# A hybrid attention and SwiGLU layer on one core: the input projection with tokens on the output partitions instead of head dimensions

## What is computed

```
h = rms_norm(x, attn_norm[l])
proj = jnp.einsum('bsd,de->bse', h, w_in[l])
mq, mk, mv, dq, dk, dv = jnp.split(proj, splits, axis=-1)
mq = rms_norm(mq.reshape(B, S, MOBA_HEADS, HEAD_DIM), moba_q_norm[l])
mk = rms_norm(mk.reshape(B, S, MOBA_HEADS, HEAD_DIM), moba_k_norm[l])
mq, mk = apply_rope(mq, cos, sin), apply_rope(mk, cos, sin)
...
x = x + jnp.einsum('bse,ed->bsd', mixed, w_out[l])
h = rms_norm(x, ffn_norm[l])
x = x + jnp.einsum('bsf,fd->bsd', jax.nn.silu(g) * u, w_down[l])
```

## Time and profile before

| what | value |
|---|---|
| three runs | 625.57 us median (624.17 to 625.68) |
| profiled execution | 624.43 us, of it 622.6 us from first to last instruction |
| granted TensorE clock, mean | 0.999, the upper of its levels |
| TensorE busy | 604.8 us (97%) |
| VectorE, ScalarE busy | 484.1 us, 311.5 us |
| attention and projection of the 8 pairs | to about 255 us of the span |

### The profile page before, as it was taken

The page is one execution under the profiler, slowest core; times in us unless marked ns, Lnnn a source line. Parts: engine busy times, 40 slices in busy tenths (PEclk is TensorE's granted clock), DMA queues, the critical chain, the costliest instruction groups (busy, mean ns, idle before and its releaser), DMA issues.

```text
span 622.6 us, 10404 instructions
## 1 busy us (share of the span) xinstructions
PE 604.8 (97%) x3774; PEld 516.1 (83%) x3774; DVE 484.1 (78%) x821; ACT 311.5 (50%) x533; POOL 28.1 (5%) x28
## 2 busy tenths in 40 slices
PE   6999999999999899999999999999999999999997
PEld 5867677776768576879999999999999998888886
DVE  4867777787687878688877887787877876999774
ACT  5354546363555454444644554536454465555551
POOL 0000000000000000000000000000000022154200
PEclk9999999999999999999999999999999999999999
DMA  8313041321404041503303432133222369699901
GB/s 318 87 65 124 1 135 24 111 67 69 124 12 136 4 164 67 177 29 138 145 26 134 137 113 91 69 136 136 80 94 99 136 158 257 189 189 207 168 35 67
DMA packets 32953, 70.31 MB, mean 113 GB/s; under 512 B 3344, under 2 KB 3728, under 8 KB 32912
## 3 DMA queue, kind: packets, MB, share of 16 engines
q1 hardware_dynamic: 26896, 58.22, 27.5%
q0 software_dynamic: 6016, 11.54, 10.5%
HBM read 63.45 MB, written 2.10 MB: 105 GB/s over the span
## 4 chain that ended last, share of the span: by engine, by line
PE 88%; DVE 7%; ACT 2%; issue 2%; DMA 1%; DVEq 0%; SPq 0%; ACTq 0%
PE ps L1472 26%; PE ps L1473 25%; PE ps L1474 25%; PE ps L1536 3%; PE ps L1549 2%; PE ps L1504 2%; PE ps L1566 1%; PE ps L1613 1%; DVE w_lo L953 1%; ACT probs L621 1%; PE ps L1574 1%; DVE w_lo L935 1%; PE ps L1795 1%; DMA ident<-ident 1%; DVE residual L1204 0%
## 5 line engine op out<-in xcount | busy, mean ns | idle before, releaser
L1472 PE MATMUL ps<-h_sum_parts,w_hi 128*128 128x256 f32 x432 | 120.6, 279 | 0.7 <-ACT q_kept L805 0.7
L1473 PE MATMUL ps<-h_sum_parts,w_hi 128*128 128x256 f32 x432 | 120.9, 280 | 0.0
L1474 PE MATMUL ps<-h_sum_parts,w_lo 128*128 128x256 f32 x432 | 120.5, 279 | 0.0
L1472 PE MATMUL ps<-h_parts,w_hi 128*128 128x512 f32 x192 | 81.5, 424 | 2.1 <-DVE h_parts L1070 1.8
L1472 PEld LDWEIGHTS ps<-h_sum_parts,w_hi 128*128 128x128 f32 x432 | 81.2, 188 | 0.9 <-ACT q_kept L805 0.9
L1473 PEld LDWEIGHTS ps<-h_sum_parts,w_hi 128*128 128x128 f32 x432 | 81.1, 188 | 0.0
L1474 PEld LDWEIGHTS ps<-h_sum_parts,w_lo 128*128 128x128 f32 x432 | 80.8, 187 | 0.0
L1474 PE MATMUL ps<-h_parts,w_lo 128*128 128x512 f32 x192 | 75.5, 393 | 0.0
L1473 PE MATMUL ps<-h_parts,w_hi 128*128 128x512 f32 x192 | 75.3, 392 | 0.0
L621 ACT ACTIVATE probs<-ps,small 128x128 f32<-128x128 f32 (+3 forms) x64 | 39.0, 614 | 51.8 <-DVE small L1016 51.8
L1472 PE MATMUL ps<-w_hi,hidden_parts 128*128 128x512 f32 x154 | 60.9, 396 | 0.0
(11 more groups left out here) (175 smaller groups left out, 1250.6 us busy)
## 6 DMA issues: line engine op xcount, KB each, us to landing
w_raw<-wt SPq DMA_DIRECT2D x61, 512.0 KB, 4.2
w_raw_odd<-wt SPq DMA_DIRECT2D x24, 512.0 KB, 4.2
w_raw_odd<-wt POOLq DMA_DIRECT2D x12, 512.0 KB, 8.5
down_raw<-wt SPq DMA_DIRECT2D x6, 512.0 KB, 11.2
w_raw<-wt POOLq DMA_DIRECT2D x5, 512.0 KB, 9.6
residual<-x SPq DMA_DIRECT2D x4, 512.0 KB, 5.0
q_rotated<-q_gained SPq DMA_DIRECT2D x32, 64.0 KB, 2.0
k_rotated<-k_gained SPq DMA_DIRECT2D x32, 64.0 KB, 2.0
```

The lines of the kernel that those rows point to most:

```text
L1472: nc.tensor.matmul(dst, lh, rh, start=start, stop=False, skip_group_check=True)
L1473: nc.tensor.matmul(dst, lh, rl, start=False, stop=False, skip_group_check=True)
L1474: return nc.tensor.matmul(dst, ll, rh, start=False, stop=stop, skip_group_check=True)
```

## The change

The projection is turned round. `project(p, tt, k)` now keeps a 128x128 piece of h (a block of 128 tokens) stationary and streams 384 weight columns, the q, k and v columns of a pair together. A pair takes 32 steps of 3 matmuls: four row blocks (`tt`) of 8 steps. Weights come in chunks of 768 numbers per partition, four to a pair, in a ring of five. The result has tokens on the partitions, so the sums of squares are a free-axis reduce on VectorE, v needs no transpose, and rotary is made with tables by token that hold the gains too. q and k are then transposed (`turn_q`, `turn_k`) and copied (`q_out`, `k_out`). The eight rotate DMAs, `mean_squares`, `spread_k`, `turn_v`, `v_scale` and the per-pair gains are gone. The filler runs about two row blocks further ahead: 18 steps of pair 1 stand before the first scores. The loops are written out. At the start x is transposed tile by tile between row blocks. Cut to its core:

```diff
+CH = KT // 2
+IN_CHUNKS = PAIRS * CH
+RING = 5
...
+def in_bank(p, tt):
+    return ((0, 1, 7, 6) if p == 0 else (0, 1, 7, 1))[tt]
...
+def chunk_load(g):
+    p, c = divmod(g, CH)
+    if g >= RING:
+        sp.wait_ge(w_lo, g - RING + 1)
+    sp.dma_start(RAWC[:, ring(g)], wt[3 * p:3 * p + 3, :, 2 * P * c:2 * P * (c + 1)].rearrange(
+        "j p n -> p j n")).then_inc(raw_c[ring(g)], 16)
...
+sp.dma_start(X[:, 0], x[0]).then_inc(x_in[0], 16)
+for g in range(CH):
+    chunk_load(g)
+for t in range(1, TT):
     sp.dma_start(X[:, t], x[t]).then_inc(x_in[t], 16)
...
+chunk_load(CH)
...
+def x_hi(tt, k):
+    act.wait_ge(x_turned, KT // 2 * tt + k // 2 + 1)
+    ins = nc.scalar.activation(H1[:, k, 0, tt * P:(tt + 1) * P], ps[:, 2 + k // 2, k % 2 * P:(k % 2 + 1) * P],
+                               ACT.Copy, scale=VEC[:, k:k + 1])
...
+def chunk_hi(g):
...
+        if c < CH - 1:
+            act.wait_ge(w_used, (CH - 1) * p + c + 1)
+        else:
+            act.wait_ge(pj_s, TT * (p + 1))
+    nc.scalar.activation(WHC[:, ring(g)].rearrange("p k (j n) -> p k j n", j=3),
+                         RAWC[:, ring(g)].rearrange("p j (k n) -> p k j n", k=2), ACT.Copy).then_inc(w_hi, 1)
...
+def qk_out(p, tt):
+    act.wait_ge(pj_s, TT * p + tt + 1)
+    if p >= 1:
+        act.wait_ge(red_s, p)
+    nc.scalar.activation(SQ[:, tt], ps[:, in_bank(p, tt), 0:2 * P].rearrange("p (j n) -> p j n", j=2),
+                         ACT.Square).then_inc(sq_s, 1)
+    if p >= 1:
+        act.wait_ge(rn_s, p)
+    nc.scalar.activation(QK[:, tt], ps[:, in_bank(p, tt), 0:2 * P].rearrange("p (j n) -> p j n", j=2),
+                         ACT.Copy).then_inc(qk_s, 1)
...
+def v_out(p, tt):
...
+    if p >= 2:
+        act.wait_ge(pv_s, p - 1)
+    nc.scalar.activation(VF[p % 2][:, tt], ps[:, in_bank(p, tt), 2 * P:3 * P], ACT.Copy,
+                         scale=XR[:, tt:tt + 1]).then_inc(v_s, 1)
...
+def q_out(t):
+    act.wait_ge(q_turn, t + 1)
+    if t >= 1:
+        act.wait_ge(sc_s, TT * t)
+    nc.scalar.activation(QF[:], ps[:, 2], ACT.Copy).then_inc(qf_s, 1)
...
+for k in range(KT):
...
+tables_out()
...
+for t in range(PAIRS - 1):
+    moba = t < MOBA_PAIRS
+    exps(t, 0, moba)
+    qk_out(t + 1, 1)
...
+    if t > MOBA_PAIRS:
+        o_squares(t - 1)
+    next_hi(t, 0)
+    exps(t, 1, moba)
...
+    exps(t, 2, moba)
+    if t + 2 < PAIRS:
+        next_hi(t, 1)
...
+        exps(t, 3, moba)
...
+    next_hi(t, 2)
+    next_hi(t, 3)
+    if t > MOBA_PAIRS:
+        mix_hi(t - 1, False)
+    qk_out(t + 1, 3)
+    v_out(t + 1, 3)
...
+    if t + 2 < PAIRS:
+        qk_out(t + 2, 0)
+    if moba:
+        mix_hi(t, True)
+    q_out(t + 1)
+    k_out(t + 1)
...
+def chunk_lo(g):
...
+    nc.vector.tensor_tensor(WLC[:, ring(g)].rearrange(view, j=3),
+                            RAWC[:, ring(g)].rearrange("p j (k n) -> p k j n", k=2),
+                            WHC[:, ring(g)].bitcast(F32).rearrange(view, j=3), ALU.subtract).then_inc(w_lo, 1)
...
+def rope(p):
+    dve.wait_ge(sq_s, TT * (p + 1))
+    nc.vector.tensor_reduce(SQS, SQ[:].rearrange("p t j (a e) -> p (t j a) e", a=2), AX.X,
+                            ALU.add).then_inc(red_s, 1)
+    dve.wait_ge(qk_s, TT * (p + 1))
...
+    nc.vector.tensor_tensor(RC[:].rearrange(heads, a=2), raw, TC[:].rearrange("p t j e -> p (t j) e").unsqueeze(
+        2).broadcast_to([P, 2 * TT, 2, HEAD]), ALU.mult).then_inc(rc_s, 1)
+    nc.vector.tensor_tensor(RN[:].rearrange(heads, a=2), raw, TS[:].rearrange("p t j e -> p (t j) e").unsqueeze(
+        2).broadcast_to([P, 2 * TT, 2, HEAD]), ALU.mult).then_inc(rn_s, 1)
+    if p >= 1:
+        dve.wait_ge(k_turn, p)
+    dve.wait_ge(rc_s, p + 1)
+    dve.wait_ge(rn_s, p + 1)
+    halves = "p t j (a h e) -> p (t j a) h e"
+    to, cos, sin = (v[:].rearrange(halves, a=2, h=2) for v in (QKR, RC, RN))
+    for h in range(2):
+        nc.vector.tensor_tensor(to[:, :, h], cos[:, :, h], sin[:, :, 1 - h], ALU.add).then_inc(rope_s, 1)
...
+def scales(p):
...
+    y = rsqrt(SQS, 16, 1.0 / HEAD, qk_newton, p, EX).rearrange("p (t j a) -> p t j a", t=TT, j=2)
+    dve.wait_ge(rope_s, 2 * (p + 1))
+    k_rows = QKR[:, :, 1].rearrange("p t (a e) -> p t a e", a=2)
+    nc.vector.tensor_tensor(k_rows, k_rows, y[:, :, 1].unsqueeze(3).broadcast_to([P, TT, 2, HEAD]),
+                            ALU.mult).then_inc(kn_s, 1)
+    if p >= 1:
+        dve.wait_ge(ex_s, p * 8)
+    nc.vector.tensor_scalar(RQ.rearrange("p (t a) -> p t a", a=2), y[:, :, 0], HEAD ** -0.5, None,
+                            ALU.mult).then_inc(rq_s, 1)
...
+tables(0)
+chunk_lo(5)
+chunk_lo(6)
+rope(0)
+chunk_lo(7)
 scales(0)
...
+for t in range(PAIRS - 1):
...
-    norm(t, 1, True)
+    next_lo(t, 0)
+    norm(t, 1, moba)
     maxima(t, 2)
...
+    if t > MOBA_PAIRS:
+        o_norm(t - 1)
+    if t + 2 < PAIRS:
+        next_lo(t, 1)
+        maxima(t, 3)
...
+    norm(t, 2, moba)
+    next_lo(t, 2)
...
+    norm(t, 3, moba)
+    next_lo(t, 3)
+    rope(t + 1)
     scales(t + 1)
...
+def project(p, tt, k):
+    g = CH * p + k // 2
+    pe.wait_ge(w_lo, g + 1)
+    if k == 0 and in_tenant(p, tt):
+        pe.wait_ge(qk_s, in_tenant(p, tt))
+        pe.wait_ge(v_s, in_tenant(p, tt))
+    if p == 0:
+        pe.wait_ge(hl, KT * tt + k + 1)
...
+        if (tt, k) == (3, 0):
+            pe.wait_ge(tab_ev, 3)
+    qs, w = slice(tt * P, (tt + 1) * P), (slice(None), ring(g), k % 2)
+    ins = product(ps[:, in_bank(p, tt), 0:3 * P], H1[:, k, 0, qs], H1[:, k, 1, qs], WHC[w], WLC[w],
+                  k == 0, k == KT - 1)
     if k == KT - 1:
+        ins.then_inc(pj_s, 1)
+    elif tt == TT - 1 and k % 2 == 1:
         ins.then_inc(w_used, 1)
...
+def turn_q(t):
+    pe.wait_ge(rope_s, 2 * (t + 1))
+    if t >= 1:
+        pe.wait_ge(ex_s, 8 * t)
...
+        ins = nc.tensor.transpose(ps[:, 2, tt * P:(tt + 1) * P], QKR[:, tt, 0], ident[:])
+    ins.then_inc(q_turn, 1)
...
+turn_gains()
+turn_x(0)
+first_rows(0, 0, 6)
+turn_x(1)
+first_rows(0, 6, KT)
+first_rows(1, 0, 6)
+turn_x(2)
+first_rows(1, 6, KT)
+turn_tables()
+first_rows(2, 0, 6)
+turn_x(3)
+first_rows(2, 6, KT)
+first_rows(3, 0, KT)
...
+fill(11)
+turn_q(0)
 fill(4)
...
+turn_k(0)
 fill(3)
...
     scores(t, 0)
-    fill(2)
-    turn_v(t)
-    fill(1)
+    fill(3 if t else 1)
     scores(t, 1)
-    turn_p(t, 0, True)
-    fill(4)
+    fill(3)
+    turn_p(t, 0, moba)
     scores(t, 2)
     fill(4)
-    turn_p(t, 1, True)
+    turn_p(t, 1, moba)
     scores(t, 3)
...
     fill(6)
-    turn_p(t, 2, True)
-    mean_squares(t + 1)
...
+    fill(3 if t < PAIRS - 2 else 2)
+    turn_p(t, 2, moba)
+    fill(4 if t < PAIRS - 2 else 2)
+    turn_p(t, 3, moba)
+    fill(3 if t < PAIRS - 2 else 2)
+    heads_out(t, 0, moba)
+    heads_out(t, 1, moba)
+    fill(2)
+    turn_q(t + 1)
+    fill(2)
+    turn_k(t + 1)
+    fill(2)
```

836 lines of the change are left out of this document (311 added, 525 removed).

## The result

The changed kernel takes **653.61 us** (median of 4 runs, 651.09 to 655.21); the kernel before, beside it on the same chip, 624.87 us (4 runs, 623.88 to 625.68). The ratio is 1.046, 95% interval 1.042 to 1.050: 28.7 us slower. The forecast was 644.0 us with a range of 630 to 652, so the direction was right and the time lies above the range. The four runs of the changed kernel spread along with their mean granted clock: 651.09 us at 0.995, 652.58 at 0.990, 654.64 at 0.986 and 655.21 at 0.984.

The account below looks back on a forecast made before the run. TensorE was taken to bind, the score-to-exponential chain right behind. Added to 624.43 us: start +9.8, pair 0 +0.7, pair 1 +0.5, pairs 2 to 4 +2.5, pair 5 +2.0, pair 6 +2.2, pair 7 +1.7: 644 us, range 630 to 652.

Parts of the forecast that it names:

- The rival in which TensorE goes on binding: Whole kernel: no waits at the scores, four pairs of 26.1 us and three of 25.3, 615 us; chance 0.10.
- The projection itself: In-projection: no change; 384 columns take 0.173 us, a pair's steps 16.6 us against 16.5.
- The rival of dearer columns: In-projection: 384 columns take 0.187 us, a step costs 0.042 us more, 652 us in all; chance 0.11.
- The removed sums: Sums of squares taken off TensorE: 1.70 us a pair, 13.6 us in eight pairs.
- A moba pair: First scores to the next pair's first scores: 28.4 us against 27.9, the saved 1.7 eaten by 2.2 of waits.
- From the fourth scores to the next pair's first ... 18.0: End of a moba pair on TensorE: 22 steps (11.4 us), 6.1 and one more transpose group (0.45), against 16.77 before.
- The start: Up to pair 0's first scores: they come at 46.1 us, 9.8 later than before.
- The wait for chunk 7: Start: VectorE runs pair 0's rotary before chunk 7's split, done at 38.7; TensorE needs it at 36.1, waits 2.6 us.
- 18 steps of lead return nothing: Pair 1 steps (9.3 us) done before the first scores return nothing until pairs 6 and 7, then meet the same chains.
- Pairs 5 to 7 and behind: Last pairs against before: pair 5 +2.0 us, pair 6 +2.2, pair 7 +1.7; nothing added after pair 7's heads.
- the term for VectorE's order: Pair 7: `mix_lo(6)` waits for `turn_o(6)` behind the fourth scores; heads at 21.5 us against 19.84 before.
- After the heads the rest is alike and moves as a block: Everything after pair 7's heads: same length as before, shift 0.

Follow-up runs that it names:

- steps dealt out otherwise: The changed kernel with the projection steps dealt 4, 5, 5, 7, 3, 3, 2, 2, 1 in a pair's gaps instead of 3, 3, 4, 9, 4, 3, 2, 2, 2: 662.96 us.
- all edits: The changed kernel with chunk 7's split earlier, steps redealt, next-pair splits earlier, and VectorE and TensorE orders changed in pairs 5 to 7: 625.17 us, ratio 1.003.
- norm of block 2 first: The changed kernel with VectorE's norm of row block 2 ahead of block 3's maxima and the split of the next pair's second chunk: 650.63 us, ratio 1.042.

## Why the prediction came out as it did

**What bounds, and the mechanism.** Right. The forecast said that the chain of score, mask, maximum and exponential would hold the scores once the filler got thin; 24 waits and 22.2 us show it. It put the fourth scores at 10.3 us into a pair; they came at 10.55. The rival in which TensorE goes on binding (pairs of 26.1) was rightly set aside, though 26.95 was reached once steps and splits were moved.

**The projection itself.** Right. Steps of three products of 384 columns start every 0.52 us (52.56 to 53.08), 0.173 a product. The rival of dearer columns is out: the 652 us that it gave lie near the measured time by accident.

**The removed sums.** Right: 1.7 us a pair forecast, 1.8 measured by doubling them, where the clock stayed up.

**A moba pair.** 28.4 us forecast, 29.06 measured; 0.65 us in each of five pairs, 3.2 in all. The failed step is "From the fourth scores to the next pair's first ... 18.0". It came to 135.78 - 117.27 = 18.51, and 0.53 of that is the wait for the chunk's split. The forecast walked VectorE's order to `turn_k`, where VectorE was in time, and never asked when TensorE's steps need each of the splits on that way. With the splits early that wait went, the stretch behind the fourth scores took 17.71 us, and a pair 28.27.

**The start.** +9.8 us forecast, +12.2 measured. The wait for chunk 7 had been seen, at 2.6 us with its end at 38.7; it was 3.12, ending at 39.6. That is 0.9 of the 2.4 missed. The other 1.55 is the lower clock behind the wait, which no term had; it came in this trace and three others, and in two with the same wait it did not. The forecast that 18 steps of lead return nothing was right as to the end (with 4 steps moved from the start into pair 7, that pair took 18.86 us for 18.85). It overlooked what the lead does in between.

**Pairs 5 to 7 and behind.** Pair 5 was right (2.0). Pair 6 measured +3.1 for +2.2, pair 7 +3.0 for +1.7: the term for VectorE's order (`mix_lo(6)` behind the fourth scores) was right in kind, since VectorE waited 5.07 us there and the reordered pair 7 took 18.85 us instead of 22.87, but it was sized too low. "After the heads the rest is alike and moves as a block" failed: +3.0 us, of which 4.64 - 2.39 = 2.25 are the heads at half clock. With the gaps filled the stretch behind was 369.6 us, as before.

**The range.** Of the 10.8 us that were missed (30.2 for 19.4), 2.4 are the start, 3.2 pairs 0 to 4, 2.2 pairs 6 and 7, and 3.0 the stretch behind the heads. The range was built from waits and column prices alone. The largest single part of what went beyond it is one thing that no case had: a kernel that waits more also runs slower for some microseconds after its longer waits. I count it at 1.55 in the start and 2.8 from the heads on by experiment; what part it has in pair 7 ahead of the heads wasn't measured by itself.

## What to carry to other kernels

A thinner filler has two schedules to meet, that of the chain it covers and that of the operands it consumes: before moving steps, list for each when its operands are ready, and move both sides together. Price each new wait of TensorE above some 1.5 us with a chance of the lower clock behind it, and where a wait can't be avoided, several short ones were better here than one long. When a block of work is given a lead, look for whose queue stands at that work's results: here that was ScalarE, whose copies ahead of an exponential made the lead necessary.

## What the runs showed of the hardware

**The clock can fall behind waits, and in busy stretches of thin products.** After waits of 3.12 us (start), 2.45 us (the kernel with steps dealt out otherwise) and the gaps of pair 7, the granted clock was 0.63, 0.61 and 0.50 for 3.5 to 4.7 us; after waits of 0.4 to 1.4 us with no longer one near them it stayed at 1.00 in every trace. It fell in or behind 3.6 to 3.8 us of two-column products without a gap as well, in six of eight cases. At the lower level a step of three products of 384 columns takes 0.96 us, so 0.32 each, which is 384 columns at 1.2 GHz. The Trainium skill, page "TensorE: Matmul & The Clock Gate", Part 1, tells of an idle engine that falls back to 1.2 GHz; the traces agree with that, and the two-column case, where the profile shows a busy engine, is one more. Behind waits it did not come every time either: behind the 3.12 us of the start in four traces of six, behind the wait of 1.56 us in pair 0 in two of six. What decides it is not shown here. The changed kernel's runs, which spread over 4 us along with their mean granted clock, fit that.

**Two paces of the same products.** In the MLP the products of 256 columns ran at one of two distances, at the same granted clock. The changed kernel and the one with all edits, ten or so products apart:

```profile
426.87 0.28 PE L1495 MATMUL ps<-h_sum_parts,w_lo 128*128 128x256 f32 x1
428.28 0.28 PE L1495 MATMUL ps<-h_sum_parts,w_lo 128*128 128x256 f32 x1
...
402.03 0.28 PE L1494 MATMUL ps<-h_sum_parts,w_lo 128*128 128x256 f32 x1
403.05 0.28 PE L1494 MATMUL ps<-h_sum_parts,w_lo 128*128 128x256 f32 x1
```

12 products in 1.41 us are 0.118 each; 9 in 1.02 are 0.113. Windows of 20 us hold 172 and 179 of them:

```profile
427.00:447.00 20.00, 20.00 (x172) 1.00 0.29 106
...
402.00:422.00 20.00, 20.00 (x179) 1.00 0.31 106
```

In both traces that had the faster pace (all edits; norm of block 2 first) it began in the middle of the stretch, some 80 to 100 us behind the MLP's first transposes, and held to its end; it saved 5.3 us. No run of the kernel before was under 623.88 us, where the faster pace would put it at 619. What sets it off stays open. It is as large as many effects that one wants to measure, so a comparison of medians within 1% needs the trace beside it.
